# Expert rows gathered in quarters and turned by VectorE, in the expert stage of a decoder step

## What is computed

```python
def hier_moe(x2d, w_rg, w_re, w1, w3, w2):
    ...
    gate = p_g[:, None] * jax.nn.softmax(top_v, axis=-1)
    expert = g_idx[:, None] * EXPERTS_PER_GROUP + top_i
    ...
    def run_block(args):
        xb, e = args
        h = jax.nn.silu(xb @ w1[e]) * (xb @ w3[e])
        return h @ w2[e]
```

## Time and profile before

| | us |
|---|---|
| median of 3 runs | 1447.11 (1442.04 to 1457.03) |
| the profiled execution, its own time | 1445.06 |
| its span, first to last instruction | 1443.2 |
| PE busy | 1306.3 (91%) |
| ACT / DVE / POOL busy | 593.5 / 578.1 / 382.2 |
| mean granted TensorE clock | 0.955 |

### The profile page before, as it was taken

The page is one execution under the profiler, slowest core; times in us unless marked ns, Lnnn a source line. Parts: engine busy times, 40 slices in busy tenths (PEclk is TensorE's granted clock), DMA queues, the critical chain, the costliest instruction groups (busy, mean ns, idle before and its releaser), DMA issues.

```text
span 1443.2 us, 20676 instructions
## 1 busy us (share of the span) xinstructions
PE 1306.3 (91%) x5827; PEld 647.7 (45%) x5828; DVE 578.1 (40%) x1787; ACT 593.5 (41%) x883; POOL 382.2 (26%) x530
## 2 busy tenths in 40 slices
PE   8999998989999988999999994999999999999800
PEld 3444435656666654455555552333333333333300
DVE  2424243635655545476676653111111111111168
ACT  0001002434445434143333321666666666666455
POOL 5113110000000001455555542123333333333134
PEclk9999999999999989999999995999999999999955
DMA  6364533222112373344553313469799888998684
GB/s 249 113 221 146 175 109 116 64 88 67 60 58 74 107 236 122 119 175 175 175 178 131 123 59 118 135 204 345 198 339 345 271 282 261 348 329 274 178 294 189
DMA packets 83135, 261.55 MB, mean 181 GB/s; under 512 B 15384, under 2 KB 34080, under 8 KB 69894
## 3 DMA queue, kind: packets, MB, share of 16 engines
q1 hardware_dynamic: 62775, 216.26, 41.6%
q0 software_dynamic: 12320, 40.93, 12.2%
q10 hardware_dynamic: 7959, 3.43, 1.0%
HBM read 202.04 MB, written 62.78 MB: 183 GB/s over the span
## 4 chain that ended last, share of the span: by engine, by line
PE 58%; issue 28%; DMA 6%; DVE 3%; ACT 2%; POOL 1%; SPq 1%; POOLq 1%; ACTq 1%; DVEq 1%
PE P L1003 12%; PE bank_S L1027 9%; PE M L1003 6%; PE bank_S L850 6%; PE P L850 5%; PE bank_S L677 4%; PE P L677 3%; PE bank_T L985 2%; PE bank_T L677 2%; PE M L677 2%; DMA work<-conv_rows 2%; PE M L868 2%; DMA big<-in_w 1%; PE M L1013 1%; DMA big<-sum_rows 1%
## 5 line engine op out<-in xcount | busy, mean ns | idle before, releaser
L1003 PE MATMUL P<-big,work 128*64 x416 | 187.0, 603 | 2.6 <-ACT work L1217 2.4
L1004 PE MATMUL P<-big,work 128*64 128x512 f32 x416 | 187.1, 603 | 0.0
L716 PE MATMUL P<-big,work 128*128 128x256 f32 (+1 forms) x512 | 173.7, 496 | 0.0
L1245 ACT ACTIVATE big<-big 128x2048 f32 x78 | 144.8, 1902 | 30.2 <-issue 16.4
L1027 PE MATMUL bank_S<-big,work 128*64 x312 | 143.6, 603 | 3.7 <-ACT big L1251 3.0
L1029 PE MATMUL bank_S<-big,work 128*64 128x512 f32 x312 | 143.6, 603 | 0.0
L716 PEld LDWEIGHTS P<-big,work 128*128 128x128 f32 x512 | 97.3, 194 | 70.4 <-issue 63.6
L850 PE MATMUL P<-big,work 128*128 128x512 f32 x256 | 116.2, 608 | 2.7 <-DVE work L1483 2.7
L1698 DVE COPY work<-M 128x256 f32<-128x256 f32 x39 | 16.6, 424 | 254.6 <-PE M L1013 254.6
L850 PE MATMUL bank_S<-big,work 128*128 128x512 f32 x256 | 113.3, 595 | 0.0
L1003 PEld LDWEIGHTS P<-big,work 128*64 128x64 f32 x416 | 55.5, 138 | 126.4 <-issue 126.4
(11 more groups left out here) (301 smaller groups left out, 2307.6 us busy)
## 6 DMA issues: line engine op xcount, KB each, us to landing
big<-in_w SPq DMA_DIRECT2D x96, 1024.0 KB, 11.8
work<-in_xt_prompt SPq DMA_DIRECT2D x32, 512.0 KB, 3.7
big<-in_toe SPq DMA_DIRECT2D x16, 512.0 KB, 3.4
work<-in_x_prompt SPq DMA_DIRECT2D x16, 512.0 KB, 4.2
h_rows<-work SPq DMA_DIRECT2D x16, 512.0 KB, 2.7
sum_rows<-work SPq DMA_DIRECT2D x16, 512.0 KB, 3.7
big<-sum_rows SPq DMA_DIRECT2D x16, 512.0 KB, 9.1
out_y_prompt<-big SPq DMA_DIRECT2D x16, 512.0 KB
```

The lines of the kernel that those rows point to most:

```text
L716: last = mm(dst[0:n, 0:c1 - c0], lhs[:, k, :], w_qkv[:, k, c0:c1], start=(k == 0), stop=(k == KD - 1))
L1003: mm(lower, xgT[:, k, 0:U], both[:, k], start=(k == 0), stop=(k == KD - 1))
L1004: last = mm(upper, xgT[:, k, U:P], w_up[:, k], start=(k == 0), stop=(k == KD - 1))
L1245: fn(w_up.rearrange("p k m f -> p m k f")[:, :, ks, :], src, ACT.Copy).then_inc(s[f"wu{part}_ok"], 1)
```

## The change

1. The list of a unit is fetched as one row of 512 bytes, copied to four partitions of `lists`, 32 apart. A new helper on DVE, `listed`, turns it in 32 x 32 pieces (`nc.vector.transpose`), works out the numbers of quarter rows (`piece_idx`, 4 times the row plus the number of the quarter of the partitions) and picks out each partition's own row and gate (`own`). It waits for the list and, from block 3 on, until the rows of the block that last used the entry of `own` have been added.
2. `gather` issues four indirect transfers a block: each brings, for 32 of the block's rows, a quarter row of 1 KB to each of the 128 partitions.
3. A new helper on DVE, `flip_rows`, turns the 128 x 1024 buffer in 32 x 32 pieces straight into `xgT`, of which there are now three. PE's `turn` and ACT's `turned` are gone.
4. `up` is cut in two halves with turn_g(b-1) between them. ACT's order becomes copy_up(b+1) first half, gated(b), copy_up(b+1) second half. The first half waits, as before, for the first half of `up(b)`.
5. SP loads w1 and w3 of the next expert when `up` of the slot's last block is done (`pe_up`), then waits for its `down` before it loads w2. Of the lists it fetches those of the first 6 blocks with ACT, before 4.
6. `y_out` becomes two semaphores by turns, so two adding transfers can be under way.
7. `keep_awake`: matmuls of constants (128 x 512, into P1, never read) at five places on PE between the last output projection and the first block: 4, 6, 3, 6 and 22 of them.
8. The scratch rows that empty slots point to are spread otherwise; six semaphores of the sample rows become one counter.

```diff
+            def keep_awake(count):
+                for _ in range(count):
+                    mm(P1[:, :], ident, C["rope"][:, 0:512], start=True, stop=True)
...
             last.then_inc(s["pe_tab"], 1)
+            keep_awake(22)
             pe.wait_ge(s["eids_ok"], 1)
...
-            def turn(b, j, i):
-                pe.wait_ge(s[f"xg_in{j}"], 16 * (i + 1))
-                after(pe, s["xgT_ev"], b - 1)
-                for k in range(KD):
-                    last = tr(T8[:, k, :], xg[j][:, k::KD], ident)
-                last.then_inc(s["pe_xg"], 1)
...
                     with pe.If(b < n_blocks):
-                        up(b, j, i)
+                        up(b, j, 0)
                     with pe.If(b - 1 < n_blocks):
                         turn_g(b - 1)
-                    with pe.If(b + 1 < n_blocks):
-                        turn(b + 1, (j + 1) % RING, i + (j + 1) // RING)
+                    with pe.If(b < n_blocks):
+                        up(b, j, 1)
                     with pe.If(b - 1 < n_blocks):
                         down(b - 1)
...
+                sp.wait_ge(s["pe_up"], done)
+                for m in range(2):
+                    load_matrix(i, q, m)
                 sp.wait_ge(s["pe_dn"], done)
-                load(i, q)
+                load_matrix(i, q, 2)
...
             for b in range(NB):
-                if b == 0:
-                    copy_up(1, (0,))
+                if b + 1 < NB:
+                    with where(b + 1):
+                        copy_up(b + 1, (0,))
                 with where(b):
                     gated(b, b % RING)
                 if b + 1 < NB:
                     with where(b + 1):
-                        turned(b + 1)
-                        copy_up(b + 1, (0, 1) if b else (1,))
+                        copy_up(b + 1, (1,))
...
+            def listed(b, j, j6, n, added=None):
+                v.wait_ge(s[f"tab_in{j6}"], 32 * (n + 1))
+                if added is not None:
+                    after(v, s[f"y_out{j6 % 2}"], added, per=16)
+                raw = view(lists[:, 2 * U * j6:2 * U * (j6 + 1)], i=2, t=32, w=2).rearrange("p i t w -> p w i t")
+                nc.vector.transpose(list_cols, raw)
+                v.drain()
+                cols = list_cols[:, :, :, 0:2].rearrange("p w i h -> p w h i")
+                ts(piece_idx[:, j], cols[:, 0], 4.0, C["quarter"], ALU.mult, ALU.add)
+                for w in range(2):
+                    tt(pick[:, w], cols[:, w], C["quad"].rearrange("p (h i) -> p h i", h=2), ALU.mult)
+                v.drain()
+                nc.vector.tensor_reduce(own[:, j6], pick.rearrange("p w h i -> p w (h i)"), AX, ALU.add).then_inc(s["tab_ok"], 1)
+
+            def flip_rows(b, j, n):
+                v.wait_ge(s[f"xg_in{j}"], 64 * (n + 1))
+                after(v, s["pe_up"], b - RING + 1)
+                nc.vector.transpose(xgT[j].rearrange("p k (i t) -> p i k t", i=4),
+                                    xg[j].rearrange("p (i f k) -> p i k f", i=4, k=KD)).then_inc(s["xgT_ev"], 1)
...
+            def gather(b, j, j6):
+                hold_ge(s["tab_ok"], b + 1)
+                hold(s["xgT_ev"], b - RING)
+                for i in range(4):
+                    g.indirect_dma_start(xg[j][:, 256 * i:256 * (i + 1)], None, h_pieces,
+                                         bass.IndirectOffsetOnAxis(ap=piece_idx[:, j, i // 2, i % 2:i % 2 + 1], axis=0)
+                                         ).then_inc(s[f"xg_in{j}"], 16)
+                gcp(idx[:, j6:j6 + 1], own[:, j6, 0:1]).then_inc(s["idx_ok"], 1)
                 hold_ge(s["idx_ok"], b + 1)
```

More of the change, by code:

```diff
@@ L94, in constants @@
     put("eps", EPS / ALPHA ** 2)
+    put("quad", (i[:, None] // 32 == np.arange(4)[None, :]).astype(np.float32))
+    put("quarter", i[:, None] // 32)
     slot = np.arange(NE + 1) % WR * WCOLS
@@ L102, in empty_slots @@
     slot = np.arange(NE * CAP)
-    spare = TOK + slot % P + slot // CAP % 2 * P
+    expert = slot // CAP
+    spare = TOK + slot % U + (expert + (expert == NE - 1) * (slot // U % 2)) % 4 * U
     return np.stack([spare, np.zeros(NE * CAP)], 1).astype(np.float32)
@@ L311, in layer @@
         xg = [take(D) for _ in range(RING)]
-        xgT = view(take(D), k=KD, t=P)
+        xgT = [view(take(D), k=KD, t=P) for _ in range(RING)]
         sg = take(FF)
@@ L317, in layer @@
         ye = take(RING * D)
-        tab = view(sb("tab", 2 * UN)[:, :], j=UN, w=2)
+        lists = take(2 * U * UN)
+        list_cols = view(take(2 * U), w=2, i=2, t=32)
+        pick = view(take(8), w=2, h=2, i=2)
+        own = view(take(2 * UN), j=UN, w=2)
+        piece_idx = view(sb("piece_idx", 4 * RING, I32)[:, :], j=RING, h=2, i=2)
         tabs = sb("tabs", 6 * NE + 8)
@@ L489, in load_matrix @@
                 sp.dma_start(wmem[:, at:at + 2 * D], src).then_inc(s[f"w{m}_ld"], 16)
-            def load(i, q):
-                for m in range(3):
-                    load_matrix(i, q, m)
             def load_conv(c):
@@ L998, in up @@
                 both = wmem[:, bass.ds(off, 2 * KD * FF)].rearrange("p (m k f) -> p k m f", m=2, k=KD)
                 lower, upper = (UP[j][h * U:(h + 1) * U, :].rearrange("p (m f) -> p m f", m=2) for h in range(2))
-                for k in range(KD):
-                    if k % (KD // 2) == 0:
-                        after(pe, s[f"wu{k // (KD // 2)}_ok"], b)
-                    mm(lower, xgT[:, k, 0:U], both[:, k], start=(k == 0), stop=(k == KD - 1))
-                    last = mm(upper, xgT[:, k, U:P], w_up[:, k], start=(k == 0), stop=(k == KD - 1))
-                    if k == KD // 2 - 1:
-                        last.then_inc(s["pe_mid"], 1)
@@ L1007, in up @@
-                last.then_inc(s["pe_up"], 1)
+                for k in range(part * KD // 2, (part + 1) * KD // 2):
+                    mm(lower, xgT[j][:, k, 0:U], both[:, k], start=(k == 0), stop=(k == KD - 1))
+                    last = mm(upper, xgT[j][:, k, U:P], w_up[:, k], start=(k == 0), stop=(k == KD - 1))
+                last.then_inc(s[("pe_mid", "pe_up")[part]], 1)
             def turn_g(b):
@@ L1036, in _ @@
                     turn_g(b - 1)
[L1037 removed]
+                up(b, b, 1)
                 if b:
@@ L1274, in _ @@
                     copy_down(b)
-                if b + RING + 1 < NB:
-                    with where(b + RING + 1):
-                        slots(b + RING + 1, (b + RING + 1) % UN)
+                if b + UN < NB:
+                    with where(b + UN):
+                        slots(b + UN, b % UN)
             with where(NB - 1):
@@ L1698, in turned, with result @@
                 cp(gT.rearrange("p k t -> p (k t)"), M0[:, 0:FF]).then_inc(s["gT_ev"], 1)
-            def result(b, j, j6):
+            def result(b, j, j6, free):
                 after(v, s["pe_dn"], b + 1)
-                after(v, s["y_out"], b - RING, per=16)
-                ts(ye[:, j * D + 512:(j + 1) * D], bank_S[:, 512:], tab[:, j6, 1:2], None, ALU.mult).then_inc(s["y_ev1"], 1)
+                if free is not None:
+                    after(v, s[f"y_out{(j6 + 1) % 2}"], free, per=16)
+                ts(ye[:, j * D + 512:(j + 1) * D], bank_S[:, 512:], own[:, j6, 1:2], None, ALU.mult).then_inc(s["y_ev1"], 1)
+            for b in range(RING):
+                listed(b, b, b, 0)
+            flip_rows(0, 0, 0)
             for b in range(UN):
```

136 lines of the change are left out of this document (74 added, 62 removed).

## The result

The changed kernel takes 1408.44 us (median of 4 runs, 1407.20 to 1410.07) against 1444.61 for the kernel before in the same series: a ratio of 0.973 (95% interval 0.967 to 0.979). Forecast were 1420 us and a range of 1399 to 1446. The time is in the range, but it lies nearer to rival A (1401) than to the forecast, two terms of the sum were off, and a stretch that had no term moved too; the errors partly cancelled. That it is 0.4 us inside the 1408 to 1432 of the forecast is luck.

A forecast was written before the change was run, and what follows sets the result against it. The prediction took PE to set the expert stage's pace, with DMA engines close behind: 1445 - 40 (PE's gain) + 19 (given back by DMA) - 4 (start) = 1420 us, range 1399 to 1446.

The forecast's parts named there:

- rival A: Whole expert stage: PE sets the pace throughout and the transfers fit; 1401 us, chance 0.22.
- PE's gain: Expert stage: removing PE's transposes saves 1.05 us a block over 38 blocks, 40 us.
- The cost of flip, list and issues: Work moved to DVE, ACT and POOL in the expert stage: hidden, taken as nothing, bounds 0 and 12 us.
- The quarters: Gathers: quarter rows as 512 packets of 1 KB cost the DMA engines 0.55 us net more a block.
- what DMA gives back: Expert stage: nearly full DMA engines take back 19 us of PE's gain, bounds 0 and 46.
- PE idle under 5 us in the stage: Sign in the expert stage that would show rival A right: PE's idle time stays under 5 us.
- the window of 403 us holds 401 of work: Rival A's condition: DMA work of 401 us fits the loading window from 906 to 1309 us.
- Rival B: Expert stage: gather packets take 0.1 us each and DMA takes back all the gain; 1440 us, chance 0.21.
- Rival C: Expert stage: gathers starve behind weight packets in load bursts, making the kernel slower; 1467 us, chance 0.09.
- The start: Before the first block: full clock and changed routing and gather work save 4 us, bounds -7 and +4.
- rival D: Start: the constants don't hold the clock; costs at most 8 us; no chance of its own given.

The follow-up runs named there:

- the idle transposes: Changed kernel with PE's eight transposes a block put back as idle work on a constant, between turn_g and the second half of up: 1447.79 us, ratio to before 1.001.
- the ballast runs: Changed kernel with an unneeded DRAM-to-DRAM copy behind each of the 28 replacing loads: 1414.10 us with 256 KB a copy, 1420.50 us with 512 KB.
- Late release: Changed kernel with the up weights again replaced only after down of the slot's last block, as before: 1420.02 us, ratio to before 0.983.
- the third edit: The change's earlier loading of w1 and w3, after up of the slot's last block; the changed kernel without it takes 1420.02 us, with it 1408.44.
- eleven variants: Follow-up programs, each the changed kernel with copies, transposes, weight release, added DMA copies, flips or constant counts altered: medians 1404.89 to 1447.79 us.
- the order of the copies alone: Kernel before with only ScalarE's first half of the next block's weight copy moved ahead of the sigmoid: 1445.71 us, ratio 1.000.
- the one with two flips: Changed kernel with VectorE turning each block's rows twice, a drain between, signalling after the second: 1409.32 us, ratio to before 0.973.
- three programs: Changed kernel with fewer constants ahead of the ranks: none (1410.93 us); 3, 4, 15 around the ranks and before block 0 (1409.25); 3, 6, 15 (1412.25).

## Why the prediction was right or wrong

**PE's gain: right in size.** 1.05 us a block was forecast, 1.01 measured in the trace; 0.87 of it is PE's own by the idle transposes, the rest was ScalarE's chain. And the condition for it was missed. "They lie on the path, since PE is never idle there" took PE for the only path. The prediction said of ScalarE "it has more room than before" and costed its part at nothing, on the sum of its work. Its room as a share was never in doubt (239 of 390 us). What counted was the one chain from the end of `up` to the first copy, which had nothing to spare in the kernel before. The order of the copies, which I charged nothing and credited nothing, is what lets most of the gain through. The change happened to have it; for this step the forecast was right by luck.

**The cost of flip, list and issues: right as zero, wrong in size.** The flip takes 2.04 us, not 1.3 (the bounds were half and three times), and twice as much of it still hides. POOL's issue is 0.96 us.

**The quarters and "what DMA gives back": the step that failed.** "It would be 512 x 0.067 = 34 us and some completion packets" took the packet for the row. (The 0.03 us for tiny packets stands in no row; the earlier trace rows give 0.009, and 1 KB would be 0.07 us by it, hardly more.) The traffic is 128 packets of 4 KB as before, plus 64 completions in place of 16: +0.09 us a block where I took 0.55. The rule of the Trainium skill that I set aside (DMA: Bandwidth & Descriptors, Specifications: at least 512 B for line rate) prices this term rightly, at nothing; its sum of 1401 is still 8 us off the profiled execution, by the start and the tail. The same page of the Trainium skill says, in the section SWDGE vs HWDGE vs iDMA, that a packet is "≤4096 B preferably" and may hold many descriptors; the trace agrees, 4 KB from four rows. The loads of the earlier trace rows go through q1, which hands over packets of 1 KB there; I carried a price from one queue to another. The conversion was too dear as well: in the ballast runs a third to two fifths of added DMA time was lost time, so by an estimate from them the 20 us that I charged would have cost 6 to 8, where the sum had 19. With this term at zero the sum is 1401; that was rival A, and its sign, "PE idle under 5 us in the stage", is met by 3.1.

**Rival A's condition** is worth a word: "the window of 403 us holds 401 of work". The work is 387 us (a DMA share of 0.90 in 905 to 1335), so there was more room than that. Late release opens the window 11 us later, counted from up(1), and costs 7.8 us in the profiled stage and 11.6 in the median: the third edit is worth some 10 us. That it works through the length of the window is argued, not shown: it also holds back the up weights of each of the 28 replaced experts from the end of an `up` to the end of its `down`, some 14 us by the rows of one block, and the ballast runs lose much less for each us of work.

**Rival B** is out with its price of 0.1 us a packet. **Rival C** asked for 32 packets an engine in each gather. They are 8 and 4 completions, and a gather lands in 6.6 us (median) in the stage; DVE's flip waits for gathered rows once, 3.2 us, at the start.

**The start: not gained.** -4 was forecast (by its own terms -4.6). 0 came in the pair of profiles: the block table 1.7 us sooner, which is within its spread, and 1.5 us more behind it. The clock does hold, against rival D, with one dip (0.84 in 870 to 880). But "22 of them take 9.5 us" was half: each is a product of 512 columns in f32 and PE makes two passes of it, 0.43 us each. (The 16 products of an `up` are 32 records in the trace of before, too.) So they run over by 5.5 us, and what the clock gave was spent.

**The tail: not foreseen.** +5.2 us after PE's last product. In the profiles of the changed kernel and of its eleven variants the tail is 76.0 to 77.0 us, with the stage of before 70.8 and 72.6 (the order of the copies alone), so it comes with the change. The place is at DVE. Its loop over the blocks goes on over blocks that don't exist here, and each such turn now tests five conditions for three. The branches of one of the five, and DVE's first work of the tail in the kernel before:

```profile
L1753 DVEq COMPARE_BRANCH  x14: 56/56/56, 1331.7 to 1346.0; - x14
```

```profile
1383.59 1.29 DVE L1727 BATCH_NORM_STATS2 work<-big 128x6 f32<-128x512 f32 x2 [10.28 <-DMA big<-sum_rows]
```

Before, DVE was through its branches 9.7 us after PE's last product, waited for the rows of the sum, and began after 11.2 us. Now the 14 empty turns keep it until 15.6 us, and it begins after 15.8 (1347.12) without a wait for data. From there on it is idle for 0.5 us until it ends the program. That is 4.6 of the 5.2 us. It is read from the traces; no run with a shorter loop tried it.

The errors of DMA (-19) on one side and of the start and the tail (+4 and +5) on the other leave 1420 - 19 + 9 = 1410, within 1 us of the profiled execution.

## What to carry to other kernels

Before work is taken off the engine that sets the pace, follow the chains that run in its shadow between two points of the period and write down what each has to spare in us; a busy share of 60% says nothing of a chain with no room left, and such an edit has to move that chain's start too, or most of it is lost. A constant distance between the end of such a chain and what it releases is a hand-over and not room: look whether it varies from block to block. Read a packet's size from the queue that will carry the transfer: small pieces of an indirect gather don't have to be small packets. Count what a new helper adds to the empty turns of a loop, if something waits behind the loop. And time a filler by rows of the same shape before its count is set, since it stands in front of the work it waits for.

## What was not expected of the hardware

- An indirect gather of 128 rows of 1 KB goes out as 32 packets of 4 KB and 16 completions; four such cost 28.8 us of engine time against 27.4 for one of 128 rows of 4 KB.
- DVE turns 128x1024 f32 in 32x32 blocks, with strided reads and writes, in 2.04 us (2029 to 2085 ns in this kernel and the one with two flips), where an arithmetic operation of as many columns takes 1.29.
- DMA work added to queues at a share of 0.96 came back as two fifths of itself in the medians (5.7 and 12.1 us for 15 and 30), and less in the profiled stage (1.9 and 8.9).
- An empty turn of DVE's loop with five conditions costs about 1.1 us (14 of them 15.4 us), though each branch is recorded with 56 ns.
- A release that no row names came 3.8 to 5.8 us late in three programs and not in others that differ from them in a few filler products.
